# A streaming-encoder block on one core: the first group's weights go to the gather ring's place, its modulation is applied by columns, and block 0's h2 is copied by DMA

## What is computed

```
h = rmsnorm(x, g1) * (1 + scale1) + shift1
qa, ka, va, qb, kb, vb, ga, gb = split(h @ w_in)
y_sb = stick_breaking_attention(qa, ka, va)          # 8 heads of 64, causal
y_sw = sliding_window_attention(qb, kb, vb, sinks)   # 8 heads, 2 kv heads, window 128
x = x + gate1 * ((sigmoid(ga) * (y_sb @ sb_proj) + sigmoid(gb) * (y_sw @ sw_proj)) @ w_out)
h2 = rmsnorm(x, g2) * (1 + scale2) + shift2
s = scores of h2 @ w_q against sub_keys              # 8 heads, 2 x 128 keys
experts, gate = top 16 of 16 x 16 sums of the two top 16      # per token and head
x = x + gate2 * sum(gate * gelu(h2 . u[experts]) * v[experts])
out = rmsnorm(x, gf)
```

## Time and profile before

| | us |
|---|---|
| median of three runs (lowest, highest) | 3668.83 (3667.49, 3670.41) |
| the profiled execution | 3687.68 |
| its span, from which all rows are | 3685.9 |

### The profile page before, as it was taken

One profiled execution on the slowest core, in us unless ns is written; L12 is line 12 of the kernel. 1 busy time (PEld: TensorE's weight loads), 2 busy tenths in 40 slices (PEclk: granted clock), 3 DMA queues, 4 the chain that ended last, 5 costly groups with the idle time before them and its releaser, 6 DMA issues.

```text
span 3685.9 us, 35795 instructions
## 1 busy us (share of the span) xinstructions
PE 2249.2 (61%) x11240; PEld 996.8 (27%) x11240; DVE 2036.1 (55%) x4768; ACT 1144.6 (31%) x3633; POOL 1121.7 (30%) x1033
## 2 busy tenths in 40 slices
PE   4678766875987856777667877684433343334333
PEld 2466623333443422223233332241000000000000
DVE  1011445657456455677577665656566656665644
ACT  1210124634213233666634213222222222222221
POOL 0000112332223323344233333333344434433432
PEclk8889868887988978888787988796555555655565
DMA  6424558888799998999899998999799989997998
GB/s 262 169 77 160 188 215 315 330 346 320 316 392 384 373 397 327 370 399 400 318 385 371 421 422 328 393 420 420 309 415 421 421 315 421 421 421 307 421 421 336
DMA packets 196264, 1276.13 MB, mean 346 GB/s; under 512 B 21261, under 2 KB 38701, under 8 KB 54633
## 3 DMA queue, kind: packets, MB, share of 16 engines
q0 software_dynamic: 147616, 1074.03, 71.8%
q1 hardware_dynamic: 48456, 199.80, 14.1%
HBM read 1249.35 MB, written 24.40 MB: 346 GB/s over the span
## 4 chain that ended last, share of the span: by engine, by line
PE 38%; DMA 33%; ACT 10%; issue 10%; DVE 6%; POOL 1%; another core or an unknown queue 1%; SPq 0%; POOLq 0%; DVEq 0%; ACTq 0%
DMA arena<-in_uv,idx_r 25%; PE pb L880 12%; PE pb L600 4%; PE pb L665 3%; ACT dg L1106 3%; PE pb L866 3%; PE pb L685 2%; PE pb L629 2%; ACT L104 2%; PE pb L603 2%; DVE arena L1411 2%; DMA arena<-in_w_q 2%; POOL arena L530 1%; PE pb L759 1%; DMA arena<-in_w_out 1%
## 5 line engine op out<-in xcount | busy, mean ns | idle before, releaser
L530 POOL DMA_INDIRECT arena<-in_uv,idx_r x1024 | 1118.6, 1092 | 2536.6 <-PE pb L880 1857.3
L1411 DVE CUSTOM_DVE_ANT_0 arena<-arena 128x1024 f32<-128x1024 f32 x1024 | 1247.8, 1221 | 719.9 <-DMA arena<-in_uv,idx_r 713.1
L880 PE MATMUL pb<-arena,dg 128*32 128x512 f32 x4096 | 745.1, 865 | 892.0 <-ACT dg L1106 842.6
L880 PEld LDWEIGHTS pb<-arena,dg 128*32 128x32 f32 x4096 | 134.6, 138 | 1395.5 <-ACT dg L1106 1033.7
L1100 ACT ACTIVATE gl<-dots 128x4 f32<-128x4 f32 x256 | 52.3, 204 | 1044.8 <-DVE dots L1411 1021.1
L665 PE MATMUL pb<-arena 128*128 128x384 f32 (+1 forms) x768 | 252.9, 487 | 57.3 <-issue 38.0
L104 ACT ACT_TABLE_LOAD x176 | 225.8, 1283 | 141.6 <-DVE dots L1411 68.4
L600 PE MATMUL pb<-arena 128*128 128x384 f32 (+1 forms) x768 | 241.5, 471 | 22.1 <-DMA arena<-in_w_mg 22.1
L1106 ACT ACTIVATE dg<-ig,gl 128x32 f32<-128x32 f32 x1024 | 245.1, 310 | 8.3
L1095 ACT ACTIVATE ig<-istack,gate_r 128x32 f32<-128x32 f32 x1024 | 241.5, 308 | 0.0
L665 PEld LDWEIGHTS pb<-arena 128*128 128x128 f32 x768 | 154.7, 206 | 150.3 <-issue 80.9
(11 more groups left out here) (153 smaller groups left out, 2239.9 us busy)
## 6 DMA issues: line engine op xcount, KB each, us to landing
arena<-in_w_mg SPq DMA_DIRECT2D x24, 1536.0 KB
arena<-in_w_ada SPq DMA_DIRECT2D x12, 2048.0 KB, 17.7
arena<-in_w_q SPq DMA_DIRECT2D x24, 1024.0 KB
arena<-in_uv,idx_r POOLq DMA_INDIRECT x1024
arena<-in_w_qk SPq DMA_DIRECT2D x12, 1024.0 KB
arena<-in_w_out SPq DMA_DIRECT2D x3, 4096.0 KB, 16.3
arena<-in_w_sw SPq DMA_DIRECT2D x3, 3072.0 KB, 13.4
arena<-in_x SPq DMA_DIRECT2D x16, 512.0 KB, 20.8
```

The lines of the kernel that those rows point to most:

```text
L530: pool.indirect_dma_start(ring[:, i % RING, :], None, uv, bass.IndirectOffsetOnAxis(ap=idx_r[:, b % 2, 4 * n + c:4 * n + c + 1], axis=0)). ...
L880: m = pe.matmul(pb[32 * c:32 * c + 32, VACC + i, :], dg[:, STEP * n // 4 % 2, c, :], ring[:, (STEP * g + c - first) % RING, D + i * HALF:D ...
L1411: dve.tensor_tensor_reduce(u, h2rep[:, c, :], u, 1.0, 0.0, ALU.mult, ALU.add, dots[:, i % 8:i % 8 + 1]).then_inc(dots_done, 1)
```

## The change

- The rounds of w_ada come in halves of k (two loads of 2 MB each), and the matmuls of a round wait for their half. Between the halves of round 0 SP issues x; behind them w_v and w_qk of pairs 0 to 2. Round 1 is computed ahead of QK of pair 0 and round 2 ahead of pair 1 (before: 1 and 3).
- shift1 and scale1 are no longer stored and loaded as rows. PE transposes md of round 0 (four transposes), VectorE copies the 16 columns to `cols`. x is multiplied by 1/rms on ScalarE (one Copy per block), transposed, and scale and shift are applied as per-partition operands when PSUM is read: four operations of 128x128 on ScalarE and four on VectorE per block, in all three groups.
- Group 0's weights lie in the ring: w_qk[1] and [2] behind wada, and once round 2 is computed w_sw at RINGO, w_mg at three places, w_out at RINGO + 12288, w_q[1] and sk. The gathers wait for the scores of heads 0 and 1 (pr_s, 4) and no longer for ada_mm.
- The first top-k takes its two heads from ssb in SBUF by two copies on VectorE. h2rep of block 0 is filled by four DMAs from h2_scratch; `replicate` runs for blocks 1 to 7.

The core of the diff:

```diff
+        def qk_home(g, p):
+            return (X0, RINGO + 16384, RINGO + 18432, L0)[p] if g == 0 else (X0, L0)[p % 2]
+        def sw_home(g):
+            return RINGO if g == 0 else W0
+        def mg_home(g, ft):
+            return RINGO + (6144, 9216, 0)[ft % 3] if g == 0 else W0 + 3072 * (ft % 2)
+        def out_home(g):
+            return RINGO + 12288 if g == 0 else A0
+        def q_home(g, h):
+            return RINGO + 3072 if (g, h) == (0, 1) else W0 + 2048 * (h % 2)
...
+                def first_weights():
+                    yield at("QK", 0, 0, 0.3)
+                    sp.wait_ge(v_mm, SIZE[0])
+                    sp.dma_start(f(qk_home(0, 3), 2048), w_qk[3]).then_inc(in_wqk[3], 16)
+                    yield at("QK", 0, 2, -1)
+                    sp.wait_ge(ada_mm, 3)
+                    sp.dma_start(f(sw_home(0), 6144), w_sw).then_inc(in_wsw, 16)
+                    sp.wait_ge(qk_mm, 2)
+                    sp.dma_start(alibi, consts[:, 2 * P + TOPK + 32:2 * P + TOPK + 32 + TABLE]).then_inc(in_alibi, 16)
+                    merge_weights(0, 0)
+                    merge_weights(0, 1)
+                    yield at("QK", 0, 3)
+                    sp.wait_ge(qk_mm, 6)
+                    sp.dma_start(f(out_home(0), 8192), w_out).then_inc(in_wout, 16)
...
+                    yield at("OUT", 0, 0, 16.5)
+                    sp.wait_ge(h2_st[0], 16)
+                    sp.wait_ge(mods_out, 128)
+                    for q in range(4):
+                        sp.dma_start(h2rep[32 * q:32 * q + 32, :, :], h2_dram[0:P, :].rearrange("(c t) n -> t c n", c=4)).then_inc(in_rep, 16)
...
-                                pool.wait_ge(ada_mm, 3)
+                                pool.wait_ge(pr_s, 4)
...
-                        yield at("H", 0, 0, -2) if r == 0 else at("QK", 0, 2 * r - 1, -0.01)
+                        yield at("H", 0, 0, -2) if r == 0 else at("QK", 0, r - 1, -0.01)
...
+                            for i in range(4):
+                                m = pe.transpose(pb[:, MISC, i * P:(i + 1) * P], md[:, 0, i * P:(i + 1) * P], ident[:])
...
+                    for j in range(GB):
+                        act.activation(xt[:, j, :], xt[:, j, :], ACT.Copy, scale=stats[:, 8 + j:9 + j]).then_inc(h_rows, 1)
...
-                        act.activation(hT[:, 0:4, j * P:(j + 1) * P], pb[:, BGB + 2 * (j % 2), :].rearrange("p (a n) -> p a n", a=4), ACT.Copy).then_inc(tr_act, 1)
+                        for k in range(4):
+                            op = act.activation(hT[:, k, j * P:(j + 1) * P], pb[:, BGB + 2 * (j % 2), k * P:(k + 1) * P], ACT.Identity,
+                                                scale=cols[:, 2 + k // 4, k % 4:k % 4 + 1], bias=cols[:, k // 4, k % 4:k % 4 + 1])
...
+                            elif g == 0 and p == 0:
+                                act.wait_ge(h2_st[0], 16)
+                                act.wait_ge(h2_st[1], 16)
...
-                        dve.wait_ge(in_tk[n % 2], 16 * (n // 2 + 1))
+                        if n == 0:
+                            dve.wait_ge(pr_se, 4)
+                            for h in range(2):
+                                step.mark(dve.tensor_copy(tk[:, 0, 256 * h:256 * h + 256].rearrange("p (q n) -> p q n", q=2), ssb[h][:, 0]))
...
-                                if n == 0:
-                                    dve.wait_ge(rep_ev, 16 * b + 4 * c + 4)
+                                if i == 0:
+                                    dve.wait_ge(in_rep, 64)
```

More of the change, by code:

```diff
@@ L355, in start, with ada @@
+                    sp.dma_start(f(W0, 4096), w_v).then_inc(in_wv, 16)
+                    for p in range(3):
+                        sp.dma_start(f(qk_home(0, p), 2048), w_qk[p]).then_inc(in_wqk[p], 16)
                     sp.dma_start(sink_row[:], sinks.partition_broadcast(P)).then_inc(in_sink, 16)
+                def ada(r, k, c):
+                    sp.dma_start(wada[:, 2 * c:2 * c + 2, 2048 * k:2048 * (k + 1)],
+                                 w_ada[4 * r + 2 * c:4 * r + 2 * c + 2, :, 4 * k:4 * (k + 1), :].rearrange("c p k n -> p c (k n)")).then_inc(in_ada[2 * k + c], 16)
@@ L360, in mods @@
                         sp.wait_ge(md_done, r + 1)
                         for c in range(4):
[L362 to L367, removed]
+                            sp.dma_start(mods_dram[4 * r + c - 4:4 * r + c - 3, :], md[32 * c:32 * c + 1, r, :]).then_inc(mods_out, 16)
@@ L425, in mixer @@
[L425 to L431, removed]
+                    if g:
+                        yield at("SWP", g, 0, -1)
+                        sp.wait_ge(pv_done, chunk(g, PAIRS - 1, 0, 0) + NC[g])
+                        if g + 1 < GROUPS:
+                            sp.wait_ge(k_st, 16 * PAIRS * (g + 1))
+                        sp.dma_start(f(sw_home(g), 6144), w_sw).then_inc(in_wsw, 16)
+                        sp.dma_start(alibi, consts[:, 2 * P + TOPK + 32:2 * P + TOPK + 32 + TABLE]).then_inc(in_alibi, 16)
+                        for ft in range(KT):
+                            yield at("MG", g, ft, -12) if ft > 1 else at("MG", g, 0, -1)
+                            if ft == 0:
+                                sp.wait_ge(ysw_mm, FIRST[g + 1])
+                            elif ft > 1:
+                                sp.wait_ge(mg_mm, 4 * (KT * g + ft - 1))
+                            merge_weights(g, ft)
@@ L506, in finals @@
                         sp.dma_start(out[b * P:(b + 1) * P, :], yfin).then_inc(stored, 16)
-                interleave(start(), mods(), mixer(0), parked(0), keys(), blocks(), finals(), *[s for g in range(1, GROUPS) for s in (mixer(g), parked(g))])
+                interleave(start(), mods(), first_weights(), mixer(0), parked(0), keys(), blocks(), finals(), *[s for g in range(1, GROUPS) for s in (mixer(g), parked(g))])
                 sp.wait_ge(stored, 16 * NB)
@@ L654, in mixer @@
                         n = HEADS * g + h
+                        wq = rows(q_home(g, h), 2 * KT, P)
                         for p in range(2):
@@ L1486 @@
     args = [nc.dram_tensor("in_" + k, v.shape, mybir.dt.from_np(v.dtype), kind="ExternalInput").ap() for k, v in arrays.items()]
-    for name, shape in (("x1_scratch", (S, D)), ("h2_scratch", (S, D)), ("mods_scratch", (12, HALF)), ("k_scratch", (PAIRS, P, S)),
+    for name, shape in (("x1_scratch", (S, D)), ("h2_scratch", (S, D)), ("mods_scratch", (8, HALF)), ("k_scratch", (PAIRS, P, S)),
                         ("v_scratch", (PAIRS, P, NB, P)), ("s_scratch", (NB, P, HEADS, 2 * NKEYS))):
```

203 lines of the change are left out of this document (123 added, 80 removed).

## The result

The median of three runs is **3573.39 us** (3572.77 to 3578.37), against 3668.83 before: a ratio of 0.9735, with a 95% interval of 0.9708 to 0.9763. The gain is 95.4 us where 100.7 was predicted; the forecast was 3568, the range 3547 to 3592. The profiled execution took 3578.4 us, its span is 3576.6. Of the executions timed for the experiments one, of the changed kernel, took 7220 us; it is left out everywhere.

What follows compares the result with a forecast made beforehand. The prediction saw a prologue of group 0 alone, with weight loads before nearly every stage, then gathers with DMA near its limit. Gains up to the first gelu summed to 100.7 us, giving 3568 from 3668.8; range 3547 to 3592.

Steps and rivals of the forecast that it cites:

- a loop that is only shifted: Gather loop from the first gelu on: costed at 0, bounds 8 us lost to 17 gained; 3159 us long as before.
- Start to V: From kernel start to the V products: V starts at 44.2 us instead of 58.75, a gain of 14.5.
- V to QK3: From V to QK of pair 3: QK3 starts at 131.6 us instead of 159.28, bringing the gain to 27.7.
- The second new wait: Pair 2's v tiles, asked for at 111.0, stand behind 7.1 MB of weights until about 124: 5.9 us.
- (b): Rival: v tiles and k/v stores wait behind prefetched weights in every pair, or the loop loses 8 us; 3583 to 3610, chance 0.18.
- SWP to PREP: From QK3 through SWP, MG and OUT to PREP: weight loads leave the path, bringing the gain from 27.7 to 63.8 us.
- w_qk[2]'s: Weights for QK of pair 2, before QK3: their 20.14 us load entry is gone because they are already in SBUF.
- PREP to the gelu: PREP to the first gelu: gain 68.0 after the top-k, then 32.7 more, mostly from the sixteen rounds, 100.7 in all.
- (c): Rival: more than summed, with waits absent, MG warm and VectorE's 12 us counting; up to 30 us, 3540 to 3553, chance 0.12.
- the 10 us: Before the first gelu: ScalarE's wait for something the profile does not name while gathers fill the DMA, assumed to stay.
- (d): Rival: the gain is given back in the loop if later stages are tied to time; 3662 to 3676, chance 0.02.
- (e): Rival: slower, TensorE granted 1.2 GHz through the prologue, 175 us added, net plus 74, 3743; chance 0.02.

Runs made afterwards that it cites:

- x_vfirst: The changed kernel with only the v tiles of pair 2 asked for ahead of w_sw, the alibi table and w_mg: 3566.78 us, ratio 0.9709.
- x_r2: The changed kernel with modulation round 2 ahead of QK of pair 2, not pair 1, and w_sw behind pair 2's v tiles: 3580.68 us, ratio 0.9712.
- x_home: The changed kernel with group 0's weights back in the places and at the times of before, except w_qk[0]: 3610.36 us, ratio 0.9816.
- x_rep: The changed kernel with block 0's copies of h2 made by sixteen rounds on TensorE and ScalarE again: 3596.34 us, ratio 0.979.

## Why the prediction was right

**The shape was right:** a prologue shortened stage by stage, and a loop that is only shifted. The gain at the gelu is 94.4 us between the two first profiles and 95.1 on one chip, and the timed one 95.4. The four parts that were put back one by one are worth 33.7 (the ring), 14.2 (the columns), 23.0 (h2rep) and 4.2 (the top-k), 75 of these 95. The other 20, the new order of w_ada's rounds above all and VectorE's passes, no run put back; they are read from the chains.

**Start to V** (44.2 predicted, 43.6 measured) was right with two errors that cancel. The passes with scale and bias take 450 ns on ScalarE and 404 on VectorE singly, eight of them 2.90 and 2.64 us, and I had 2.0: "0.45 ACT L1023 x2" in the earlier trace rows are two that overlap, with no pointer operands, and I halved them. The view of one line shows the single ones:

```profile
L1001 ACT ACTIVATE arena<-pb,cols x32: 437/450/487, 40.5 to 1287.7; 128x128 f32<-128x128 f32 x32
```

The transposes of x were under the cover of VectorE's passes over md (1.97 us for 16, not 3.0), which gave it back. The estimate from the Trainium skill ("ScalarE: Activation LUTs", Rules for kernel authors), 0.41 us each, was nearer than my row. The same page ("What ACT_TABLE_LOAD costs") says that each pointer operand adds 93 ns to 186 plus 0.833 per column, and that such passes in sequence overlap by 93: an estimate of 0.48 singly and 0.39 in sequence, where this trace has 0.45 and 0.36.

**V to QK3 is the step that was off.** "SP can ask for it only behind md_done and four stores of mods, at 69.6; 23.2 us later is 92.8. This is a new wait, 5.8 us inside the round, with QK1 queued behind it: QK1 at 96.3". The wait is there, with its cause and its place. It was mis-sized: round 1's second half came 1.9 later (65.3, not 63.4), so SP asked at 71.4; the load took 24.4 us; and the second half, after 6.29 us of idle, ran at 6.50 instead of 3.5. QK1 started at 102.3, 6.0 us late: 1.8, 1.2 and 3.0. The missing term is the third: the granted clock was 0.55 in that half (95.8 to 102.3 us) and 1.00 in the first (85.9 to 89.5). I had charged a cold start to V and to the first round, and left it out behind the wait that I had just put in. That 6.0 is so near the 6.3 by which the whole sum is short is luck, as what lies behind cancels: QK3 was 8.1 late, PREP 4.6, the first gather 4.4 and the gelu 6.3.

The second new wait was right in place and size (5.9 predicted; 5.9 gone at SWP in x_vfirst). Rival (b) speaks of stores of k behind weights, but not of the one behind w_ada as next in line: x_r2 shows it.

**SWP to PREP.** From QK3 to PREP's start I had 195.4 us (327 less 131.6); it took 191.9, where before took 231.5. QK3 and its attention took 14.7 and not 16.3, SWP 14.03 for 64 and not 16.92, MG and OUT started with no load in the chain. By x_home the loads from w_sw to sk are worth 30.5 to 32.8 from SWP to the gelu. By itself this part came out 3.5 us better than forecast. The loads from w_sw to sk were right; the one wrong attribution is w_qk[2]'s, told there; its size was in the sum.

**PREP to the gelu**: h2rep by DMA is worth 23.0 to 24.4 us (x_rep), the larger part of the 32.7, and the rest I put down to VectorE's passes, which no run isolated. The first top-k is worth 4.2 to 4.5 (4.2 predicted). From the first gather to the gelu it took 50.7 us where I had 48.8: the list behind the load of x has no transposes of it, and they stand in the chain (1.95 us at 423.86). The h2 store's wait, costed at nothing, is in no chain of the changed kernel.

**The rivals.** (b) did not come: the waits are the two forecast, 6.3 and 6.0 us (the one for the v tiles by the view of their line). Of (c) one term came: MG starts warm (7.17 for its first 32 and not 9.22). The second wait, the 10 us and the loop's length stayed. (d) has fallen. (e) has fallen as well: the window from 0 to 433 us has TensorE at a granted clock of 0.89 of the full 2.4 GHz, against 0.84 in the 527 us before.

The two windows, before and after:

```profile
0.00:527.00 527.00, 350.22 (x1712) 249.73 (x1712) 107.12 (x276) 82.75 (x231) 12.56 (x19) 0.84 0.46 173
```

```profile
0.00:433.00 433.00, 328.41 (x1588) 241.90 (x1588) 98.65 (x283) 85.96 (x233) 12.55 (x19) 0.89 0.55 209
```

## What to carry to other kernels

Where a stage waits for its weights in the chain, a place that is free early can remove the whole wait (here from w_sw to sk), but every load moved ahead in a shared queue is a debt: list the small transfers that now stand behind it (v tiles, stores that free a buffer) and put those first. Where you put a wait inside a run of matmuls, charge the cold half behind it too. Split a measured gain at one mark (here the first gelu) and compare the part behind it on one chip before you explain a few us of it.

## What the runs showed of the hardware

- A small transfer on SP's queue lands late behind large ones: a 128x256 store of k took 2.2 us at the least, 7.4 in the median and 19.6 behind 8.4 MB; v tiles 13.0 us behind 7.1 MB.

```profile
L476 SPq DMA_DIRECT2D k_scratch<-arena x8: 319/320/344, 76.5 to 648.0; - x8
...
DMA to landing us min/median/max: 2.2/7.4/19.6
```

The Trainium skill ("DMA: Bandwidth & Descriptors", Queues, rings and completion order) says that each DMA engine takes descriptors in ring order; these late landings fit it.

- Loads on SP's queue share the DMA with GpSimd's gathers: 1 MB of w_q took 9.9 us while ten gathers of 1 MB ran, and 5.3 to 5.6 in the four loads before them; with the gathers held back x took 16.2 instead of 9.5.
- Half a round of modulation (x32 in a row of the timeline) takes 3.64 us behind other work at a granted clock of 1.00, 6.50 after 6.29 us of idle at 0.55, and 6.13 after 6.94 at 0.58. The very first half took 5.55 us though the view grants 1.00 there (19.2 to 24.75 us), which no run explains.
- The granted clock at one place of one program differs between executions: ahead of MG it was 0.60 in the first profile of the changed kernel and 1.00 in the two others, and from SWP to MG they took 54.0, 51.0 and 51.2 us.
